# State outputs among the third level's products, merges over four quarters of TensorE, and state sums among right-hand sides, in a fused RWKV-7 and window-attention kernel

## What is computed

```
S = S * w_t + (S @ -kk_t) (kk_t * a_t)^T + v_t k_t^T      # decay, removal, new pair
y_t = S @ r_t
```

## Time and profile before

| | us |
|---|---|
| median of three runs (3101.14 to 3106.66) | 3101.15 |
| the profiled execution | 3103.45 |
| its span | 3101.6 |
| TensorE matmul busy (share of the span) | 2881.4 (93%) |
| VectorE busy | 1603.5 (52%) |
| ScalarE busy | 1082.7 (35%) |
| GpSimd busy | 619.5 (20%) |

### The profile page before, as it was taken

One profiled execution on the slowest core, in us unless ns is written; L12 is line 12 of the kernel. 1 busy time (PEld: TensorE's weight loads), 2 busy tenths in 40 slices (PEclk: granted clock), 3 DMA queues, 4 the chain that ended last, 5 costly groups with the idle time before them and its releaser, 6 DMA issues. The chain is left out here.

```text
span 3101.6 us, 77931 instructions
## 1 busy us (share of the span) xinstructions
PE 2881.4 (93%) x34698; PEld 2361.3 (76%) x34698; DVE 1603.5 (52%) x2628; ACT 1082.7 (35%) x2003; POOL 619.5 (20%) x417
## 2 busy tenths in 40 slices
PE   7999999999878888888888999999999999999899
PEld 4887888887467777777787778888877887777677
DVE  5533232432267777777763663222377304777762
ACT  4223332322645445454453441001122113556310
POOL 5522222210023232232321120000000001332320
PEclk9999999999989999999998999999999999999999
DMA  5123331211653232332306763111111226225472
GB/s 174 62 78 116 104 107 48 95 48 57 214 152 98 79 105 74 96 97 78 108 18 191 225 181 83 34 41 41 40 63 62 89 90 232 71 90 180 155 247 85
DMA packets 342221, 326.15 MB, mean 105 GB/s; under 512 B 14159, under 2 KB 254159, under 8 KB 341248
## 3 DMA queue, kind: packets, MB, share of 16 engines
q1 hardware_dynamic: 313296, 261.72, 27.9%
q10 hardware_dynamic: 24480, 47.21, 4.3%
q0 software_dynamic: 4112, 12.25, 1.5%
HBM read 203.18 MB, written 122.64 MB: 105 GB/s over the span
## 5 line engine op out<-in xcount | busy, mean ns | idle before, releaser
L331 PE MATMUL pj_ps<-pj_x_hi,pj_w_hi 128*128 128x512 f32 x1024 | 402.7, 393 | 11.4 <-DVE pj_w_lo L280 6.7
L331 PE MATMUL pj_ps<-pj_x_hi,pj_w_lo 128*128 128x512 f32 x1024 | 400.0, 391 | 0.0
L331 PE MATMUL pj_ps<-pj_x_lo,pj_w_hi 128*128 128x512 f32 x1024 | 400.0, 391 | 0.0
L2017 PE MATMUL dm_ps<-h_hi,dm_w_hi 128*128 128x512 f32 x896 | 279.5, 393 | 0.0
L2017 PE MATMUL dm_ps<-h_hi,dm_w_lo 128*128 128x512 f32 x896 | 275.9, 389 | 0.0
L2017 PE MATMUL dm_ps<-h_lo,dm_w_hi 128*128 128x512 f32 x896 | 275.8, 389 | 0.0
L221 POOL TENSOR_TENSOR pj_x<-h 128x512 f32<-128x512 f32 x128 | 166.9, 1305 | 487.3 <-DVE pj_x_lo L275 438.8
L275 DVE TENSOR_TENSOR pj_x_lo<-pj_x,pj_x_hi 128x512 fp32r<-128x512 f32 x128 | 91.6, 715 | 321.5 <-ACT pj_x_hi L350 321.3
L331 PEld LDWEIGHTS pj_ps<-pj_x_hi,pj_w_hi 128*128 128x128 f32 x1024 | 193.2, 189 | 55.4 <-DVE pj_w_lo L280 9.3
L331 PEld LDWEIGHTS pj_ps<-pj_x_lo,pj_w_hi 128*128 128x128 f32 x1024 | 193.4, 189 | 41.3 <-issue 1.0
L331 PEld LDWEIGHTS pj_ps<-pj_x_hi,pj_w_lo 128*128 128x128 f32 x1024 | 193.2, 189 | 40.5
(11 more groups left out here) (268 smaller groups left out, 5893.4 us busy)
## 6 DMA issues: line engine op xcount, KB each, us to landing
proj<-pj_out ACTq DMA_DIRECT2D x128, 256.0 KB, 2.5
pj_w<-w_in SPq DMA_DIRECT2D x32, 512.0 KB, 4.3
proj<-lr_out SPq DMA_DIRECT2D x32, 512.0 KB, 5.8
dm_w<-w_out SPq DMA_DIRECT2D x32, 512.0 KB, 5.3
dm_w<-w_in SPq DMA_DIRECT2D x30, 512.0 KB, 4.9
partial<-wa_ob SPq DMA_DIRECT2D x48, 264.0 KB, 2.2
mo_part<-partial SPq DMA_DIRECT2D x16, 792.0 KB, 9.1
wa_vt<-v_rows SPq DMA_DIRECT2D x44, 260.0 KB, 3.2
```

The lines of the kernel that those rows point to most:

```text
L331: mm = pe.matmul(ps[i][:], wp, xp, start=k == 0 and m == 0, stop=k == KT - 1 and m == len(parts) - 1)
L2017: last = pe.matmul(PS[:, 2 * i + b, :], wp, hp[:, k, t0:t0 + 512], start=k == 0 and m == 0, stop=k == KT - 1 and m == len(parts) - 1)
```

## The change

`home(ci, l)` gives the half in which level `l` keeps chunk `ci`: its own half at level 1, the other half at levels 2 to 5. Products of a level write to the half `home(ci, l)`. Merges read there; they write X to the half of the chunk and Y to the half where the next level wants it. In levels 1 to 4 X and Y so use different quarters, and they are issued pair by pair. In level 3 each state output of tile `b` (`y_of`) is issued ahead of the two products with the same `g` and `j`. The state sums of the first chunk (`m_of`) and the right-hand sides of the second (`z_of`) are issued in turns in `m_and_z`. The number of matmuls stays the same.

```diff
--- before.py
+++ after.py
@@ -787,6 +787,10 @@
 
         chunk = rows
 
+        def home(ci, l):
+
+            return chunk(ci if l == 1 else 1 - ci)
+
         def bank(b, w):
 
             return PS[:, b, :].rearrange("p (j w) -> p j w", w=w)
@@ -1290,7 +1294,7 @@
                     at = C_AT["selectT"] + 128 * i
                     return cst[P, at:at + 128]
 
-                def products(f, l, b=None):
+                def products(f, l, b=None, beside=None):
                     for g in range(2):
                         if l == 1:
                             f.need("turned", g + 1)
@@ -1299,10 +1303,12 @@
                         else:
                             f.need("xy_sb", 2 * (l - 2) + g + 1)
                         for j in range(KT):
+                            if beside:
+                                beside(g, j)
                             for ci in range(NCH):
                                 R = chunk(ci)
-                                last = pe.matmul(bank(XB[g], CHUNK)[R, j, :], lt_less[R, g, j, :], x16[R, g, j, :],
-                                                 start=True, stop=True, skip_group_check=True)
+                                last = pe.matmul(bank(XB[g], CHUNK)[home(ci, l), j, :], lt_less[R, g, j, :],
+                                                 x16[R, g, j, :], start=True, stop=True, skip_group_check=True)
                         f.did(last, "w")
 
                 def merges(f, l):
@@ -1310,14 +1316,13 @@
                         f.need("w_sb", 2 * (l - 1) + g + 1)
                         for j in range(KT):
                             for ci in range(NCH):
-                                R = chunk(ci)
-                                pe.matmul(bank(XB[g], CHUNK)[R, j, :], y16[R, g, j, :], w16[R, g, j, :],
+                                R = home(ci, l)
+                                pe.matmul(bank(XB[g], CHUNK)[chunk(ci), j, :], y16[R, g, j, :], w16[R, g, j, :],
                                           start=True, stop=True, skip_group_check=True)
-                        for j in range(KT):
                             for ci in range(NCH):
-                                R = chunk(ci)
-                                last = pe.matmul(bank(YB[g], CHUNK)[R, j, :], w16[R, g, j, :], y16[R, g, j, :],
-                                                 start=True, stop=True, skip_group_check=True)
+                                R = home(ci, l)
+                                last = pe.matmul(bank(YB[g], CHUNK)[home(ci, l % 5 + 1), j, :], w16[R, g, j, :],
+                                                 y16[R, g, j, :], start=True, stop=True, skip_group_check=True)
                         f.did(last, "xy")
 
                 def residual(f):
@@ -1381,25 +1386,47 @@
                                              start=first and j == 0, stop=True, skip_group_check=True)
                     return last
 
+                def y_of(b, ci, j):
+                    for g in range(2):
+                        last = pe.matmul(bank(4 + ci, CHUNK)[rows(g), j, :], state(b.t, ci)[rows(g), j, :],
+                                         ar[b.t % 2][rows(g), j, ci, CHUNK:128], start=False, stop=True,
+                                         skip_group_check=True)
+                    return last
+
                 def y_from_state(b):
                     b.need("yu")
                     for j in range(KT):
                         for ci in range(NCH):
-                            for g in range(2):
-                                last = pe.matmul(bank(4 + ci, CHUNK)[rows(g), j, :], state(b.t, ci)[rows(g), j, :],
-                                                 ar[b.t % 2][rows(g), j, ci, CHUNK:128], start=False, stop=True,
-                                                 skip_group_check=True)
+                            last = y_of(b, ci, j)
                     b.did(last, "y")
 
+                def z_of(f, ci, j, g):
+                    R = chunk(ci)
+                    return pe.matmul(bank(ZB, RW_N)[rows(g), j, :], mat_k[f.t % 2][R, g, j, 0:CHUNK],
+                                     v_tok[f.t % 2][R, j, rows(g)], start=j == 0, stop=True, skip_group_check=True)
+
+                def m_of(f, ci, j, g):
+                    R = chunk(ci)
+                    return pe.matmul(bank(MB, RW_N)[rows(g), j, :], b_tok[R, j, rows(g)], u_tok[f.t % 2][R, g, j, :],
+                                     start=False, stop=True, skip_group_check=True)
+
                 def z_from_values(f, ci):
-                    R = chunk(ci)
-                    if ci:
-                        f.need("z_sb", ci)
                     for j in range(KT):
                         for g in range(2):
-                            last = pe.matmul(bank(ZB, RW_N)[rows(g), j, :], mat_k[f.t % 2][R, g, j, 0:CHUNK],
-                                             v_tok[f.t % 2][R, j, rows(g)], start=j == 0, stop=True, skip_group_check=True)
+                            last = z_of(f, ci, j, g)
                     f.did(last, "zv")
+
+                def m_and_z(f):
+                    f.need("u_sb0", 1)
+                    f.need("u_sb1", 1)
+                    f.need("z_sb", 1)
+                    for j in range(KT):
+                        m_of(f, 0, j, 0)
+                        z_of(f, 1, j, 1)
+                        m = m_of(f, 0, j, 1)
+                        z = z_of(f, 1, j, 0)
+                    f.did(m, "m")
+                    f.did(z, "zv")
 
                 def z_from_state(f, ci):
                     f.need("zv", ci + 1)
@@ -1442,13 +1469,11 @@
                         at.did(sums_by_head(sq, 6), "ksum")
 
                 def m_from_solved(f, ci):
-                    R = chunk(ci)
                     f.need("u_sb0", ci + 1)
                     f.need("u_sb1", ci + 1)
                     for j in range(KT):
                         for g in range(2):
-                            last = pe.matmul(bank(MB, RW_N)[rows(g), j, :], b_tok[R, j, rows(g)],
-                                             u_tok[f.t % 2][R, g, j, :], start=False, stop=True, skip_group_check=True)
+                            last = m_of(f, ci, j, g)
                     f.did(last, "m")
 
                 def a_products(n, i):
@@ -1481,10 +1506,20 @@
                     if n:
                         n.need("kinv")
                         n.did(spread(sel_t, kinv, 6), "kspread")
-                    if b:
+                    if b and f:
+                        b.need("yu")
+
+                        def state_part(g, j):
+                            last = y_of(b, g, j)
+                            if g and j == KT - 1:
+                                b.did(last, "y")
+
+                        products(f, 3, None, state_part)
+                    elif b:
                         y_from_state(b)
-                    if f:
+                    elif f:
                         products(f, 3)
+                    if f:
                         merges(f, 3)
                         if n:
                             n.need("kk")
@@ -1530,8 +1565,7 @@
                             f.need("bv")
                         a_products(n, 1)
                     if f:
-                        m_from_solved(f, 0)
-                        z_from_values(f, 1)
+                        m_and_z(f)
                     if n:
                         n.need("kt")
                         n.need("a_sb", 2)
```

More of the change, by code:

```diff
@@ L1483, in step @@
                         n.did(spread(sel_t, kinv, 6), "kspread")
-                    if b:
+                    if b and f:
[6 more added lines that the diff above has]
+                    elif b:
                         y_from_state(b)
+                    elif f:
+                        products(f, 3)
                     if f:
-                        products(f, 3)
                         merges(f, 3)
```

## The result

The changed kernel is slower: 3118.99 us median of six runs (3104.71 to 3132.64), against 3102.85 (3100.44 to 3106.66) of the kernel before on the same chips. The ratio is 1.0056 with a 95% interval of 1.0033 to 1.0078, some 16 us. Its profiled execution is the slowest of the six, 3132.64 us with a span of 3130.9, so its rows show the cause larger than the median has it.

What follows compares the result with a forecast made beforehand. It took TensorE's waits for its own code to bound the recurrence. Sums (-3.3 us), level 2 merges (-2.2) and late outputs (+2.2) gave -3.3 us, from 3101.15 to 3097.9 us, range 3085 to 3109.

Steps and rivals of the forecast that it cites:

- Level 1 ... Worth nothing: Level 1 merges: 0.27 us saved a group, but the next TensorE work waits 0.70 us for the key matrix.
- Levels 3 and 4 ... Worth nothing: Merges of levels 3 and 4: the ScalarE, not the merges, sets when levels 4 and 5 start; no gain.
- rival C: TensorE's clock falls more often as gaps behind the sums grow: 13.6 us more, 3111.5 us; chance 0.08.
- Rival D: Merges writing one PSUM bank from two halves stay at 16 ns; level 2's 2.2 us gone, 3100.1; chance 0.06.
- B's mechanism: Mixed stretch of level 3: a code piece's border delays state outputs and the ScalarE; 7.7 us, 3108.9 us; chance 0.14.
- the 0.13 us that I took: Forecast's loss a tile from later state outputs in the mixed stretch, 2.2 us in all; bounds 0 and 7.7 us.
- B's 0.48 us: Delay of the state outputs in every tile if they end where the products ended; 7.7 us over 16 tiles.
- A's full gain: Code is no floor: level 2 and the sums save 0.27 + 0.82 us a tile, 17.4 us, 3083.7; chance 0.22.
- My net gain of 3.3 us: Whole change: sums save 3.3 us, level 2 saves 2.2, late outputs cost 2.2.
- gaps at issue would grow by 10 us or more: Sign of the main step: TensorE's idle time at issue over the recurrence grows by some 10 us or more.
- 3.95 us is no floor of a piece of code: Recurrence: the prediction claimed TensorE can't finish a piece of 128 matmuls in less than some 3.95 us.

Runs made afterwards that it cites:

- merges_only: Kernel before with the four-quarter merges alone, state outputs and state sums apart: 3109.1 against 3101.76 us, ratio 1.0016.
- after_fill2: Changed kernel plus 14 wide filler matmuls a tile (512 columns, results unused) in the waits of the levels: 3098.52 against 3103.96 us, ratio 0.9986.
- sums_only: Kernel before with only the state sums issued among the second chunk's right-hand sides: 3099.43 against 3101.76 us, ratio 0.9985.
- before_fill2: Kernel before plus the same 14 wide filler matmuls a tile in the waits: 3099.13 against 3103.96 us, ratio 0.9990.
- outputs_only: Kernel before with the new halves and state outputs mixed with level 3's products; merges at the old pace, sums apart: 3116.4 against 3101.76 us, ratio 1.0041.
- merges_sums: Changed kernel without the mixed outputs; four-quarter merges and mixed sums stay: 3108.4 against 3105.65 us for the kernel before, ratio 1.0013.
- less_code: Kernel before with 28 of 32 matmuls of one right-hand-side group left out, so it computes something else: 3090.24 against 3103.96 us, 0.9966.

## Why the prediction was wrong

**The step that failed** is the one that counted a wait at nothing. "Level 1 ... Worth nothing", "Levels 3 and 4 ... Worth nothing": that holds for the path, and the rows after bear it out, since the waits of the levels took up what the merges saved. But TensorE idle in more places fell to 1.2 GHz more often, and the price of that was no term of my sum. I had it as rival C, with a chance of 0.08, and with the wrong place: I wrote that the gaps that would grow lie behind the sums. They grew in the levels (L1320, L1310, L1385), and 19 of the 29 falls begin there, against 4 of 16 before. I had also sized C too small: one more fall of 3.4 us in every second tile is 27 us more at the lower clock, and the profiled execution has 163 - 74 = 89 us more. C's time was 3111.5 us; measured are 3118.99, or 16.1 us over before.

**The size of it.** The mean clock went from 0.972 to 0.961, which is 0.011/0.5 x 3101 = 68 us more at the lower level. The 99 runs of the unchanged kernel in the three sets differ in clock from run to run by themselves; a straight line through each set gives 17, 13 and 22 us for each 0.01. For 0.011 that is 14 to 24 us. So the clock can carry the whole 16 us. This line is a correlation; that the clock is the cause rests on wide against narrow fillers, and on the change with and without fillers at equal clock. The line doesn't hold for every kernel: for merges_only it gives 13 to 22 us, and 5 were measured.

**What was right.** Merges at 8 ns, mixed outputs in the time of the outputs alone, sums and right-hand sides in 0.94 us. Rival D (one bank from two halves) is out, as the merges reached four-quarter pace. B's mechanism is there, as 8 of 14 tiles have late outputs, but small: 0.2 us a tile against 0.1 us before is near the 0.13 us that I took and far under B's 0.48 us, and after_fill2 rules it out as the cause of the loss. A's full gain for the sums is out by sums_only; for level 2 it wasn't tested.

**What was not borne out.** My net gain of 3.3 us is not shown: at equal clock (after_fill2 against before_fill2) the medians differ by 0.6 us and the ratios by 0.04%, with intervals of about 0.17% to either side. That gaps at issue would grow by 10 us or more was too much: 64.9 against 59.6. And 3.95 us is no floor of a piece of code. The pieces are real: in the kernel before, each gap at issue over 0.3 us in the recurrence ends a multiple of 126 to 128 matmuls behind the last one (43 distances; the two gaps of the earlier trace rows are 127 apart by the rows). But the 13 single pieces among them took from 3.48 to 7.67 us from gap to gap, so the time of a piece isn't fixed.

**What stays open.** How the loss divides between merges and outputs: alone they gave 1.0016 and 1.0041, together with the sums 1.0056, with overlapping intervals. Why outputs_only loses more than merges_only at a higher clock (0.965 against 0.962), and the changed kernel more than merges_sums at nearly the same, is not explained. With the fillers that difference is gone, so it may be that late outputs cost time only where the clock is low, or that the falls then lie where they cost more; neither was tested. That waits for code are why the edits gain so little is supported by less_code, not proved.

## What to carry to other kernels

A faster matmul in a stretch where TensorE waits for other engines can save nothing there and cost the clock of the stretch behind it, where TensorE is the bound. So price two things for every edit that thins TensorE's work: the path, and the granted clock of the stretches around it. A clock theory is tested by wide matmuls put into the waits, against the same instructions with few columns. And a comparison at equal clock needs the fillers in both kernels: here only that showed that the edits gain nothing measurable by themselves.

## What the runs showed of the hardware

- TensorE's clock fell behind idle time spread over several short waits: the last three ahead of the fall shown were of 0.54, 0.79 and 0.54 us. The fall of the earlier trace rows stood behind one gap, of 3.40 - 1.89 = 1.51 us. The Trainium skill (TensorE: Matmul & The Clock Gate, Why this matters for your kernels) warns of long idle gaps between bursts of matmuls. The trace agrees that idle time lowers the clock, and shows that it need not be one long gap.
- 128x128 by 512 float16 matmuls in the waits, 8 a tile, took the clock of the recurrence to 0.94, where 8 columns in place of 512 left it at 0.90.
- Merges whose operands lie in different partition halves, and that write the same PSUM bank in different partition halves, ran at 8 ns a matmul (32 started within 0.25 us), all four quarters at once.
- There was one packet of the instruction queue for about 253 instructions of TensorE (164 packets in 740 us of the changed kernel, for 20,756 matmuls and 20,752 weight loads). Gaps at issue stood one or more pieces of 126 to 128 matmuls apart. Those of a single piece were 3.93 and 4.02 us apart in the earlier trace rows, and from 3.48 to 7.67 us elsewhere in the kernel before.
